# A hybrid encoder layer on one core: the second column half of the output projection, by token tile instead of by weight tile

## The reference

```python
x = x + 0.5 * swiglu(rms_norm(x, p['ffn1_norm']), p['ffn1_w_gu'], p['ffn1_w_down'])
h = rms_norm(x, p['mix_norm'])
proj = h @ p['w_in']          # then gated DeltaNet (o_gdn) and differential attention (o_diff)
mixed = jnp.concatenate([o_gdn, o_diff.reshape(B, L, DIFF_V).astype(o_gdn.dtype)], axis=-1)
x = x + mixed @ p['w_out']
x = x + 0.5 * swiglu(rms_norm(x, p['ffn2_norm']), p['ffn2_w_gu'], p['ffn2_w_down'])
```

## Time and profile before

| | |
|---|---|
| median of 3 runs | 1523.1 us (1522.17 to 1531.36) |
| the profiled execution | 1521.75 us |
| its span, first to last instruction | 1519.9 us |
| PE busy | 1406.2 us (93%) |
| the output projection's products on PE | 1004.22 to 1063.12 us |
| first product of the second FFN on PE | 1072.38 us |

### The profile page before, as it was taken

The page is one execution under the profiler, slowest core; times in us unless marked ns, Lnnn a source line. Parts: engine busy times, 40 slices in busy tenths (PEclk is TensorE's granted clock), DMA queues, the critical chain, the costliest instruction groups (busy, mean ns, idle before and its releaser), DMA issues.

```text
span 1519.9 us, 24379 instructions
## 1 busy us (share of the span) xinstructions
PE 1406.2 (93%) x8685; PEld 1261.7 (83%) x8685; DVE 925.5 (61%) x1499; ACT 675.7 (44%) x1267; POOL 373.7 (25%) x248
## 2 busy tenths in 40 slices
PE   4899999999997999899989988689699999999999
PEld 4899999988886998787877665467599999998887
DVE  4977667744446766647635665633687766764444
ACT  5555555533335543434243332432555555543332
POOL 0655555500000000312022221000355555530000
PEclk9899999999998999999998999799899999999999
DMA  4222222270101422111130026660122222226000
GB/s 164 80 88 83 83 83 83 83 290 0 28 0 37 144 61 82 56 32 53 47 108 1 1 78 196 214 219 1 56 84 84 83 83 83 83 85 247 0 35 35
DMA packets 139254, 127.27 MB, mean 84 GB/s; under 512 B 3781, under 2 KB 107845, under 8 KB 139196
## 3 DMA queue, kind: packets, MB, share of 16 engines
q1 hardware_dynamic: 136684, 117.15, 24.1%
q0 software_dynamic: 2512, 9.34, 1.8%
HBM read 115.83 MB, written 10.39 MB: 83 GB/s over the span
## 4 chain that ended last, share of the span: by engine, by line
PE 84%; DVE 10%; ACT 3%; issue 2%; DMA 1%; POOL 0%; SPq 0%; DVEq 0%; ACTq 0%
PE psum_all L892 22%; PE psum_all L893 22%; PE psum_all L894 22%; PE psum_all L902 6%; PE psum_all L1750 2%; PE psum_all L1997 1%; PE psum_all L1763 1%; DVE hw_lo L328 1%; PE psum_all L2000 1%; PE psum_all L1866 1%; PE psum_all L468 1%; PE psum_all L1755 1%; DMA K_c<-cache_k 1%; PE psum_all L2123 0%; DVE gu_op L552 0%
## 5 line engine op out<-in xcount | busy, mean ns | idle before, releaser
L892 PE MATMUL psum_all<-hw_hi,gu_op 128*128 128x320 f32 x1224 | 384.7, 314 | 20.4 <-DVE gu_op L552 12.0
L893 PE MATMUL psum_all<-hw_lo,gu_op 128*128 128x320 f32 x1224 | 381.4, 312 | 0.0
L894 PE MATMUL psum_all<-hw_hi,gu_op 128*128 128x320 f32 x1224 | 381.0, 311 | 0.0
L892 PEld LDWEIGHTS psum_all<-hw_hi,gu_op 128*128 128x128 f32 x1224 | 234.2, 191 | 21.8 <-issue 17.2
L893 PEld LDWEIGHTS psum_all<-hw_lo,gu_op 128*128 128x128 f32 x1224 | 234.3, 191 | 0.0
L894 PEld LDWEIGHTS psum_all<-hw_hi,gu_op 128*128 128x128 f32 x1224 | 233.8, 191 | 0.0
L552 DVE TENSOR_TENSOR gu_op<-w_sum,gu_op 128x512 fp32r<-128x512 f32 x168 | 167.3, 997 | 58.9 <-ACT gu_op L548 53.6
L769 POOL TENSOR_TENSOR w_sum<-raw_gu 128x512 f32<-128x512 f32 x84 | 144.6, 1722 | 229.5 <-DVE gu_op L552 224.8
L892 PE MATMUL psum_all<-wd_hi,a_hi 128*128 128x512 f32 x440 | 171.4, 390 | 1.7 <-DVE x_tok L910 1.7
L893 PE MATMUL psum_all<-wd_lo,a_hi 128*128 128x512 f32 x440 | 171.2, 389 | 0.0
L894 PE MATMUL psum_all<-wd_hi,a_lo 128*128 128x512 f32 x440 | 171.2, 389 | 0.0
(11 more groups left out here) (341 smaller groups left out, 2451.8 us busy)
## 6 DMA issues: line engine op xcount, KB each, us to landing
raw_gu<-ffn_w_gu SPq DMA_DIRECT2D x84, 512.0 KB, 4.6
wd<-ffn_w_down SPq DMA_DIRECT2D x2, 4096.0 KB, 21.1
raw_b<-w_in SPq DMA_DIRECT2D x8, 1024.0 KB, 5.2
K_c<-cache_k SPq DMA_DIRECT2D x8, 1024.0 KB, 8.0
V_c<-cache_v SPq DMA_DIRECT2D x8, 1024.0 KB, 5.6
wd<-ffn_w_down SPq DMA_DIRECT2D x2, 3584.0 KB, 12.5
raw_cv<-w_in SPq DMA_DIRECT2D x13, 512.0 KB, 4.1
wd<-ffn_w_down SPq DMA_DIRECT2D x6, 1024.0 KB, 5.0
```

The costliest lines, as they stand in the source:

```text
L892: nc.tensor.matmul(out, lhs_hi, rhs_hi, start=start, stop=False, skip_group_check=True)
L893: nc.tensor.matmul(out, lhs_hi, rhs_lo, start=False, stop=False, skip_group_check=True)
L894: return nc.tensor.matmul(out, lhs_lo, rhs_hi, start=False, stop=stop, skip_group_check=True)
```

## The change

The first column half stays as it is, step by step over k. The second half goes token tile by token tile: for each t, all eight k with three matmuls each. For this all eight weight tiles of half 1 must be split at once, so seven of them go to new buffers `keep_o0` to `keep_o6` (which lie over `z`, `q_tok` and the front of the first raw weights) and the eighth to `o_hi[:, 0]`, `o_lo[:, 0]`. The list `SPLITS` puts the splits of half 1 between those of half 0. The products of t = 0 go to bank 7, the next ones to banks 0 and 1 in turn (`late_bank`); a bank is used again after the residual that reads it. `norm_pe` of token tile t - 1 stands on PE behind the products of token tile t (t = 1, 2, 3). ACT's and DVE's norm of tiles 0 to 2 goes one tile after the other (`in_turn`). `mixed` lies tile by tile (`mixed_hi`, `mixed_lo`: 4096 bytes of a partition for each token tile) in the region in which `hT_hi`, `hT_lo` lay, over which the FFN's operands are written.

```diff
-            square(0)
-            square(1)
-            root(0)
-            square(2)
-            root(1)
-            root(2)
-            columns(0, 4)
+            if in_turn:
+                square(0)
+                root(0)
+                square(1)
+                root(1)
+                columns(0, 2)
+                square(2)
+                root(2)
+                columns(2, 4)
+            else:
+                square(0)
+                square(1)
+                root(0)
+                square(2)
+                root(1)
+                root(2)
+                columns(0, 4)
             token_hi(act, f, 0)
...
-            residual(0)
-            residual(1)
-            inverse(0)
-            residual(2)
-            inverse(1)
-            dve.wait_ge(gain_ready, 16)
-            scale(0)
-            inverse(2)
-            scale(1)
-            scale(2)
-            residual(3)
+            if in_turn:
+                dve.wait_ge(gain_ready, 16)
+                for t in range(3):
+                    residual(t)
+                    inverse(t)
+                    scale(t)
+            else:
+                residual(0)
+                residual(1)
+                inverse(0)
+                residual(2)
+                inverse(1)
+                dve.wait_ge(gain_ready, 16)
+                scale(0)
+                inverse(2)
+                scale(1)
+                scale(2)
+                residual(3)
             token_lo(dve, f, 0)
             token_lo(dve, f, 1)
+            if in_turn:
+                residual(3)
             token_lo(dve, f, 2)
             token_lo(dve, f, 3)
             ahead(dve)
...
+        over_h = Region(nc, h_at, h_end)
+        mixed_hi = over_h.put("mixed_hi", [P, TT, KT, P], F32R)
+        mixed_lo = over_h.put("mixed_lo", [P, TT, KT, P], F32R)
...
-            part = which[:, 4 * half:4 * half + 4, t * P:(t + 1) * P]
+            part = which[:, t, 4 * half:4 * half + 4, :]
...
+        SPLITS = [(0, 0), (0, 1), (0, 2), (1, 0), (0, 3), (1, 1), (0, 4), (1, 2), (0, 5), (1, 3),
+                  (0, 6), (1, 4), (0, 7), (1, 5), (1, 6), (1, 7)]
+        NTH_SPLIT = {split: n + 1 for n, split in enumerate(SPLITS)}
+        keep_o = [nc.alloc_sbuf_tensor_at(f"keep_o{k}", [P, 2, BANK], F32R, offset=at)
+                  for k, at in enumerate([F0 + 4096 * i for i in range(5)] +
+                                         [tok_at + 4096 * i for i in range(2)])]
+
+        def out_weights(half, k):
+
+            if half and k < KT - 1:
+                return keep_o[k][:, 0], keep_o[k][:, 1]
+            return o_hi[:, 0 if half else k % 2], o_lo[:, 0 if half else k % 2]
 
         def wout_act(act):
             for n in range(TT):
                 out_act(act, n)
-            for n in range(2 * KT):
-                half, k = n // KT, n % KT
-                if n == 2:
-                    finish(diff_out_act(act, 1))
-                for m in BEHIND.get(n - 2, ()):
-                    out_act(act, m)
+            for half, k in SPLITS:
+                if half == 0:
+                    if k == 2:
+                        finish(diff_out_act(act, 1))
+                    for m in BEHIND.get(k - 2, ()):
+                        out_act(act, m)
+                    if k >= 2:
+                        act.wait_ge(N["wo_step"], k - 1)
+                elif k == 0:
+                    act.wait_ge(*on.tr(2 * TT))
+                elif k >= 5:
+                    act.wait_ge(N["wo_lo"], NTH_SPLIT[0, k if k == KT - 1 else 4])
+                    if k == KT - 1:
+                        act.wait_ge(N["wo_step"], KT - 1)
                 act.wait_ge(s_wo[half], 16)
-                if n >= 2:
-                    act.wait_ge(N["wo_step"], n - 1)
-                nc.scalar.activation(o_hi[:, n % 2], raw_o[half][:, k, :], ACT.Copy)\
+                nc.scalar.activation(out_weights(half, k)[0], raw_o[half][:, k, :], ACT.Copy)\
                     .then_inc(N["wo_hi"], 1)
 
         def wout_dve(dve):
             for n in range(TT):
                 out_dve(dve, n)
-            for n in range(2 * KT):
-                half, k = n // KT, n % KT
-                if n == 2:
-                    finish(diff_out_dve(dve, 1))
-                for m in BEHIND.get(n - 2, ()):
-                    out_dve(dve, m)
+            for n, (half, k) in enumerate(SPLITS):
+                if half == 0:
+                    if k == 2:
+                        finish(diff_out_dve(dve, 1))
+                    for m in BEHIND.get(k - 2, ()):
+                        out_dve(dve, m)
                 dve.wait_ge(N["wo_hi"], n + 1)
-                V.tensor_tensor(o_lo[:, n % 2], raw_o[half][:, k, :], raw(o_hi[:, n % 2]),
-                                ALU.subtract).then_inc(N["wo_lo"], 1)
-                if n == KT + 1:
-                    dve.wait_ge(N["x_back"], 32)
-                    for t in range(TT):
-                        wout_residual(dve, 0, t)
+                hi, lo = out_weights(half, k)
+                V.tensor_tensor(lo, raw_o[half][:, k, :], raw(hi), ALU.subtract)\
+                    .then_inc(N["wo_lo"], 1)
+            dve.wait_ge(N["x_back"], 32)
+            for t in range(TT):
+                wout_residual(dve, 0, t)
 
         def wout_residual(dve, half, t):
             if half == 0:
@@ -2413,30 +2455,40 @@
             else:
                 dve.wait_ge(N["wo_out"], t + 1)
             cols = x_tok[:, t, half * BANK:(half + 1) * BANK]
-            V.tensor_tensor(cols, psum[(half * TT + t) % 8], cols, ALU.add).then_inc(N["wo_res"], 1)
+            V.tensor_tensor(cols, psum[late_bank(t) if half else t], cols, ALU.add)\
+                .then_inc(N["wo_res"], 1)
+
+        def late_bank(t):
+
+            return (7, 0, 1, 0, 1)[t]
 
         def wout_pe(pe):
             for n in range(TT):
                 out_pe(pe, n)
-            for n in range(2 * KT):
-                half, k = n // KT, n % KT
-                if n == 0:
+            for k in range(KT):
+                if k == 0:
                     pe.wait_ge(*on.lo(TT))
-                elif n == KT // 2:
+                elif k == KT // 2:
                     pe.wait_ge(*on.lo(2 * TT))
-                pe.wait_ge(N["wo_lo"], n + 1)
+                pe.wait_ge(N["wo_lo"], NTH_SPLIT[0, k])
+                hi, lo = out_weights(0, k)
                 for t in range(TT):
-                    c = slice(t * P, (t + 1) * P)
-                    if k == 0 and half == 1 and (TT + t) % 8 < TT:
-                        pe.wait_ge(N["wo_res"], (TT + t) % 8 + 1)
-                    last = three(psum[(half * TT + t) % 8], hT_hi[:, k, c], hT_lo[:, k, c],
-                                 o_hi[:, n % 2], o_lo[:, n % 2], k == 0, k == KT - 1)
-                    if n == 2 * KT - 1:
-                        last.then_inc(N["wo_out"], 1)
-                if n < 2 * KT - 1:
-                    last.then_inc(N["wo_step"], 1)
-                for m in BEHIND.get(n, ()):
+                    last = three(psum[t], mixed_hi[:, t, k], mixed_lo[:, t, k], hi, lo, k == 0,
+                                 k == KT - 1)
+                last.then_inc(N["wo_step"], 1)
+                for m in BEHIND.get(k, ()):
                     out_pe(pe, m)
+            for t in range(TT):
+                if t:
+                    pe.wait_ge(N["wo_res"], (0, 1, 2, TT + 2, TT + 3)[t])
+                for k in range(KT):
+                    if t == 0:
+                        pe.wait_ge(N["wo_lo"], NTH_SPLIT[1, k])
+                    last = three(psum[late_bank(t)], mixed_hi[:, t, k], mixed_lo[:, t, k],
+                                 *out_weights(1, k), k == 0, k == KT - 1)
+                last.then_inc(N["wo_out"], 1)
+                if 1 <= t <= 3:
+                    norm_pe(pe, f2.n, (t - 1,), f2.hx)
...
             wout_pe(pe)
-            norm_pe(pe, f2.n, range(3), f2.hx)
             ffn_pe(pe, f2)
```

More of the change, by code:

```diff
@@ L328, in token_lo, with ffn_norm_act @@
             nc.vector.tensor_tensor(lo, src, raw(hi), ALU.subtract).then_inc(s.hl.sem, 1)
-        def ffn_norm_act(act, f, x_ready, ahead):
+        def ffn_norm_act(act, f, x_ready, ahead, in_turn=False):
             s = f.n
@@ L363, in ffn_norm_act, with ffn_norm_dve @@
             token_hi(act, f, 5)
-        def ffn_norm_dve(dve, f, gain_ready, residual=lambda t: None, ahead=lambda dve: None):
+        def ffn_norm_dve(dve, f, gain_ready, residual=lambda t: None, ahead=lambda dve: None,
+                         in_turn=False):
             s = f.n
@@ L2370, in out_act @@
             act.wait_ge(*on.tr(n + 1))
-            nc.scalar.activation(out_hT(hT_hi, n), out_psum(n), ACT.Copy).then_inc(on.hi.sem, 1)
+            nc.scalar.activation(out_hT(mixed_hi, n), out_psum(n), ACT.Copy).then_inc(on.hi.sem, 1)
         def out_dve(dve, n):
             dve.wait_ge(*on.hi(n + 1))
-            V.tensor_tensor(out_hT(hT_lo, n), out_psum(n), out_hT(raw(hT_hi), n),
```

(8 more changed lines are left out.)

## The result

| | before | changed |
|---|---|---|
| median, us (runs) | 1525.74 (20) | 1516.18 (20) |
| lowest to highest | 1521.91 to 1533.13 | 1511.57 to 1522.73 |
| profiled execution | 1521.75 | 1515.08 |

The ratio is 0.9938, 95% interval [0.9923, 0.9953]: 9.5 us less, between 7.2 and 11.7. The interval leaves out "no change", but the gain is under the 1% that the prediction counted as a difference; the forecast of the gain was 9.9 us. The forecast time, 1512.5, lies 3.7 us under the measured median: over 20 runs the median of before is 2.6 us above that of the three runs it was made from, the forecast was set 0.7 us under the median of those three less 9.9, and the gain is some 0.3 us smaller.

A forecast was written before the change was run, and what follows sets the result against it. TensorE bounds the kernel, busy 1406.2 of 1519.9 us, so time lies where it idles or runs slow. Gains of 7.2 and 2.75 us make 9.9 at tile 4's transposes; forecast 1512.5 us, range 1508.5 to 1517.5.

The forecast's parts named there:

- that case: Whole kernel: the change gains as summed, 9.9 us, giving 1509 to 1514 us; chance 0.70.
- the longer cold stretches: After PE's two later waits: low clock could last 6.35 us each; gain only 4.5 to 8, 1514 to 1518; chance 0.16.
- Product A earlier: Second FFN's first product: starts at 1065.2 instead of 1072.38, 7.2 us gained.
- Product A at full clock: Second FFN's first product: without 3.54 us idle before it, takes 3.60 us instead of 6.35, 2.75 us more gained.
- Tile 3's handover: After the second FFN's first product: tile 3's scaled row is ready at 1068.7, just in time for the product's end, 1068.8.
- The norm is hidden: Output projection's second half: each tile's norm, 3.8 us, fits under 5.6 us of products; PE waits at no transposes.
- PE full from 1000 to 1063: Output projection: PE is full at clock 1.00 in this stretch of the kernel before.
- Splits ahead at nothing: Half 0 of the output projection: early weight splits cost nil, covered by its matmuls; the last is done by 1033.
- The tie at step k = 3: Half 0: DVE delivers at 1016.85, PE asks at 1016.93; cost taken as 0, upper end 0.3 us.
- Slower: the clock drops: Second half: transposes between products could take the clock to 1.2 GHz, 21.5 us more, time 1536; chance 0.04.
- The stretch behind shifts as a whole: From tile 4's transposes on: everything comes 9.9 us earlier, with PE's 5.12 us wait and later low clock unchanged.

The follow-up runs named there:

- the clock alone: The kernel before, with 14 throwaway 512-column matmuls in PE's idle time before the second FFN's product A: 1520.06 us (6 runs), ratio 0.9953.
- the splits ahead alone: The changed kernel with the second half's products step by step over k and the norm as before; weights still split early: 1523.64 us, ratio 1.0001.
- the kernel with the pieces: The changed kernel with the second FFN's operands for tokens 320 to 639 made in pieces of 192 and 128 tokens: 1516.83 us, ratio 0.9939.
- order alone: The changed kernel with tiles 0 to 2's transposes behind all products and the norm's staggered order on ACT and DVE: 1522.27 us, ratio 0.9978.
- ACT's repeated square: The changed kernel with ACT's row squaring repeated for tiles 0 to 2, once (1514.64 us, single run) or three times (1517.62 us, ratio 0.9948).
- the change once more: The changed kernel, unedited, measured and profiled a second time: 1517.57 us (6 runs), ratio 0.9947 against the kernel before.
- POOL behind the split: The changed kernel with POOL's first difference of the second FFN made to wait for DVE's split h_lo: 1520.51 us (9 runs), ratio 0.9954.
- the warm PE: The changed kernel with 32 and 34 throwaway matmuls in PE's two waits behind tile 4's transposes: 1516.7 us (4 runs), ratio 0.9914.

## Why the prediction was right, step by step

- *The time.* The gain is the one summed up; the time, 1516.18 us, is not in the 1509 to 1514 of that case but in the 1514 to 1518 of the longer cold stretches, and 1.3 us inside the upper end of the range. It got there because three runs of before had given a median 2.6 us too low, not by that rival's mechanism. That the width of the range, made for other reasons, took this in was luck.
- *Product A earlier.* Forecast 60.98 after the mark, measured 61.11; 7.05 us of the 7.2. All products of the half at 0.235 us, the three groups 0.8 us each, no wait: held.
- *Product A at full clock.* 1071.96 - 1068.42 = 3.54 us against 3.60; the gain of 2.75 is shown by itself (2.74 from the clock alone). The profile of before happened to have nearly the whole product cold; with the splits ahead alone it was 4.89 us, and the term would have been 1.3.
- *Tile 3's handover.* Forecast 0.1 us of slack, measured 0.06.
- *The norm is hidden.* 3.81 us for 3.8, and the cover was measured from both sides (4.9 us fits, 7.0 does not).
- *PE full from 1000 to 1063.* It was full from the first product on; the 34.60 us that begin at 1000 hold 31.85 us of work, and the missing 2.75 us are the wait before that product. Nothing in the sum hangs on it.
- *Splits ahead at nothing.* The last ends at 1035.79, mark 28.5, forecast 28.8, and no product waits for one. The tie at step k = 3 fell well: DVE delivers at mark 12.65 (forecast 12.63) and PE asks at 12.82.
- *Slower: the clock drops.* It stayed 1.00 with 24 transposes between the products, and even with gaps of 1.63 us among them. The rule of the Trainium skill weighed above ("TensorE: Matmul & The Clock Gate", section "Part 4: PE-mode transpose"), that the full clock does not engage for transposes, is not borne out for groups of eight between products, where the granted clock was 1.00; a stretch of transposes alone was not tried.
- *The stretch behind shifts as a whole.* Held to 0.13 us, but for a reason that the prediction did not see. It took the low clock after the waits for a cost, and priced longer cold stretches at 2.3 us. One did come longer (0.69 for 0.84), and cost nothing, because DVE beside POOL sets the time up to the next restart. In the rival of longer cold stretches, the price was wrong for this one: it was read from PE's rows alone. A low clock behind the third wait, which the prediction did not consider, goes with 2.7 us more in the kernel with the pieces. In the change that wait is 0.57 us and the clock behind it 1.00, which no step of the prediction had foreseen: in this the shift went well by luck.

The forecasts of two experiments were off in size: order alone gains 3.2 and not 2.0 us, and ACT's repeated square is 1.08 us and not 1.3.

## What to carry to other kernels

A reduction over a whole row can stand behind the next tile's products if the loop is turned so that tiles finish one by one; compare its chain, read from one tile's rows, with one tile's products, and count the clock that comes back where the gap closes. Before a cold stretch is priced, look who ends the wait behind it: if it is another engine that works on without waiting for PE, as behind the first wait here, PE's clock there is free; where PE's own work follows without a gap, as before product A, it costs its full price. And when an engine's wait is shortened by moving a neighbour, look at what the neighbour meets next.

## What was not expected of the hardware

- DVE and POOL hold each other up, up to about twofold, where both work on SBUF: DVE's split of 1280 elements takes 1.49 us with POOL idle and 3.05 beside it, the pair of 512-element weight splits 3.98 us or 6.70, by what POOL does meanwhile, and POOL's difference of 1280 elements took 2.88 us in the change and 4.00 where it met DVE's own difference. What a shift of POOL gave to one DVE operation here it took from another. The rows look like turns and not like a shared rate. POOL's row in the change, beside the pair `gu_op`:

```profile
1093.19 3.96 POOL L808 TENSOR_TENSOR hx<-hx,hT 128x1280 f32<-128x1280 f32 x1
```

It ends at 1097.15, and PE, which waits for the first of the pair, goes on at 1097.85, 0.70 us later; a weight split by itself takes 0.68 to 0.69. In the profiles of before, of the change once more, of POOL behind the split and of the pieces, PE's second restart likewise comes 0.69 or 0.70 us behind the end of a difference of POOL, with the warm PE 0.60. So it is POOL's difference that sets this restart. This is read from rows; no run was made for it.
- The same loop has two paces. The second and the last of 21 rows of one kind of DVE in the FFN's loop, in the change and then in its second profile:

```profile
1125.24 0.49 DVE L719 TENSOR_TENSOR aT<-aT,psum_all 128x320 f32<-128x320 f32 x1
...
1359.32 0.49 DVE L719 TENSOR_TENSOR aT<-aT,psum_all 128x320 f32<-128x320 f32 x1 [1.70 <-PE psum_all L914]
```

```profile
1123.50 0.49 DVE L719 TENSOR_TENSOR aT<-aT,psum_all 128x320 f32<-128x320 f32 x1
...
1356.39 0.49 DVE L719 TENSOR_TENSOR aT<-aT,psum_all 128x320 f32<-128x320 f32 x1 [1.68 <-PE psum_all L914]
```

That is 234.08 and 232.89 us for the same instructions, at a granted clock of 1.00 in the one's loop as in the other's. PE is busy all the time in both, so it is PE's own pace: 1597 matmuls in 234.0 or in 232.9 us. It makes up nearly all of the 1.3 us between the two groups of spans above. The kernel with the pieces, though its way to the end is 436.98 us, runs this loop at the faster pace (232.89 us). The cause is open.
- The start of the output projection lies anywhere from 1004.22 to 1009.75 us in eleven profiles, with nothing changed ahead of it but where five pieces are written. A change worth a few microseconds is seen in marks long before it is seen in one span.
